# A hybrid streaming encoder step on one core: the last pass over the output visits its tiles in another order, and its norm begins before the pass is over

## The reference, cut to what matters

```
def _rmsnorm(x, g):
    y = xf * lax.rsqrt(jnp.mean(xf * xf, axis=-1, keepdims=True) + EPS)
    return (y * g.astype(jnp.float32)).astype(x.dtype)

    h = _rmsnorm(x, norm1_g) * (1.0 + sc1) + sh1
    mix, new_state = _token_mixers(h, ...)          # h @ w_in, three attentions
    x = x + g1 * (mix @ w_out)
    h = _rmsnorm(x, norm2_g) * (1.0 + sc2) + sh2
    x = x + g2 * (jnp.square(jax.nn.relu(h @ w_up)) @ w_down)
    ...
y_prompt = _rmsnorm(xp, final_g)
```

## Time and profile before

| | us |
|---|---|
| median of 3 runs | 3301.9 (3301.85 to 3302.01) |
| profiled execution | 3300.42 |
| its span | 3298.6 |
| TensorE busy in the span | 3211.7 |
| VectorE busy | 1694.6 |
| ScalarE busy | 984.2 |
| GpSimd busy | 959.5 |

### The profile page before, as it was taken

One profiled execution on the slowest core, in us unless ns is written; L12 is line 12 of the kernel. 1 busy time (PEld: TensorE's weight loads), 2 busy tenths in 40 slices (PEclk: granted clock), 3 DMA queues, 4 the chain that ended last, 5 costly groups with the idle time before them and its releaser, 6 DMA issues.

```text
span 3298.6 us, 50329 instructions
## 1 busy us (share of the span) xinstructions
PE 3211.7 (97%) x19286; PEld 2889.6 (88%) x19286; DVE 1694.6 (51%) x3073; ACT 984.2 (30%) x1770; POOL 959.5 (29%) x690
## 2 busy tenths in 40 slices
PE   6999999999999999999999999999999999999998
PEld 2988898667899999999988879966678999999997
DVE  4746273774485555555663544056546533333335
ACT  3132222764451111111232213157535211111112
POOL 1312333221233333333331215213113233333331
PEclk8999999999999999999999999999999999999999
DMA  5512477545022222222222115554321111111112
GB/s 215 181 43 86 163 240 227 116 111 140 26 71 84 78 88 76 76 83 89 83 65 67 38 47 186 185 144 102 78 70 42 33 46 45 48 47 45 45 45 72
DMA packets 135350, 307.07 MB, mean 93 GB/s; under 512 B 53788, under 2 KB 74340, under 8 KB 131728
## 3 DMA queue, kind: packets, MB, share of 16 engines
q1 hardware_dynamic: 93584, 224.39, 23.3%
q10 hardware_dynamic: 41600, 80.44, 6.9%
HBM read 240.14 MB, written 57.90 MB: 90 GB/s over the span
## 4 chain that ended last, share of the span: by engine, by line
PE 92%; DVE 3%; ACT 1%; ACTq 1%; DMA 1%; issue 1%; POOL 0%; SPq 0%; DVEq 0%; POOLq 0%; PEldq 0%
PE ps L1400 22%; PE ps L1371 19%; PE ps L1312 9%; PE ps L1245 8%; PE ps L1035 6%; PE ps L1225 5%; PE ps L1091 4%; PE ps L1182 3%; PE ps L1289 3%; PE ps L1347 2%; PE ps L1017 2%; PE ps L1059 1%; DVE tn L2066 1%; PE ps L1080 1%; DVE h_lo L2079 1%
## 5 line engine op out<-in xcount | busy, mean ns | idle before, releaser
L781 POOL CAST w_hi<-raw 128x1024 fp32r<-128x1024 f32 x212 | 231.1, 1090 | 1858.5 <-PEq L1406 447.2
L2251 DVE SCALAR_TENSOR_TENSOR x<-ps,mod,x 128x352 f32<-128x352 f32 (+2 forms) x768 | 353.6, 489 | 431.5 <-PE ps L1400 351.5
L1400 PE MATMUL ps<-act_hi,w_hi 128*128 128x352 f32 x1536 | 496.0, 323 | 0.0
L1400 PE MATMUL ps<-act_hi,w_lo 128*128 128x352 f32 x1536 | 492.6, 321 | 0.0
L1400 PE MATMUL ps<-act_lo,w_hi 128*128 128x352 f32 x1536 | 492.1, 320 | 0.0
L1888 ACT ACTIVATE relu_b<-ps,consts 128x352 f32<-128x352 f32 x192 | 106.3, 554 | 1103.5 <-PE ps L1371 1084.4
L1371 PE MATMUL ps<-h_hi,w_hi 128*128 128x352 f32 x1344 | 433.5, 323 | 0.0
L1371 PE MATMUL ps<-h_hi,w_lo 128*128 128x352 f32 x1344 | 430.8, 321 | 0.0
L1371 PE MATMUL ps<-h_lo,w_hi 128*128 128x352 f32 x1344 | 430.4, 320 | 0.0
L1312 PE MATMUL ps<-pT,vb 128*128 128x512 f32 (+5 forms) x1080 | 395.7, 456 | 0.0
L2315 DVE TENSOR_REDUCE pm<-ps 128x1 f32<-128x512 f32 (+4 forms) x468 | 250.2, 547 | 228.3 <-PE ps L1182 144.1
(11 more groups left out here) (223 smaller groups left out, 6095.1 us busy)
## 6 DMA issues: line engine op xcount, KB each, us to landing
raw<-in_w SPq DMA_DIRECT2D x212, 512.0 KB, 3.6
ada_next<-in_w_ada SPq DMA_DIRECT2D x48, 512.0 KB, 4.2
ada_w<-in_w_ada SPq DMA_DIRECT2D x24, 512.0 KB, 4.8
kb<-scr_k SPq DMA_DIRECT2D x36, 328.0 KB
kb<-scr_k SPq DMA_DIRECT2D x120, 82.0 KB
qb<-scr_q SPq DMA_DIRECT2D x36, 264.0 KB
ada_nat<-in_w_ada_first SPq DMA_DIRECT2D x8, 1024.0 KB, 20.4
qb<-scr_q SPq DMA_DIRECT2D x120, 66.0 KB
```

The costliest lines, as they stand in the source:

```text
L781: pool.tensor_copy(hi, raw[:, uc % 2, 0:width]).then_inc(pool_hi, 1)
L1400: last = mm(ps[:, i % 6, 0:GW], w[:, k * 256 + o * 128:k * 256 + o * 128 + 128], (act_lo if low else act_hi)[:, k * T + g * GW:k * T + (g ...
L2251: last = v.scalar_tensor_tensor(xs, ps[:, bank, a - g * GW:b - g * GW], gs, xs, ALU.mult, ALU.add)
```

## The change

The output projection and the last down of each layer use a new order of tiles, `LAST_ORDER`: after blocks 0 to 3, blocks 4 to 7 of group 0 (tiles 12 to 15), then blocks 4 and 5 of groups 1 and 2 (16 to 19), then blocks 6 and 7 of groups 1 and 2 (20 to 23). Group 0 is thus complete at tile 15 instead of 19. TensorE makes its mean of squares behind tile 17 instead of 21, and those of groups 1 and 2 inside the next stage's first group of matmuls. VectorE makes the scalings 0 to 2 and low halves 0 and 1 between the residuals of tiles 19 to 23 (or, after the last layer, six final scalings, and two more around the last add). Weight units are released behind tiles 6, 12, 20 instead of 6, 12, 18, and the unit of blocks 6 and 7 is first used at tile 14 instead of 18. Slots 2 and 5 of the first MLP chunk's units 43 and 44 are exchanged, and GpSimd's split of unit 45 waits for the eighth low half. The modulation products of the last chunk stand at other tiles, its scales at tiles 10 and 12 instead of 15.

```diff
+LAST_ORDER = ([(b, g) for b in range(4) for g in range(GROUPS)] + [(4, 0), (5, 0), (6, 0), (7, 0), (4, 1), (5, 1), (4, 2), (5, 2)] +
+              [(6, 1), (7, 1), (6, 2), (7, 2)])
+RELEASED_AT = (6, 12, 20)
...
-           [2, 0, 1, 2] + [0, 1, 2, 0] + [1, 2, 5, 0, 1, 2, 0, 1])
+           [2, 0, 1, 2] + [0, 1, 2, 0] + [1, 5, 2, 0, 1, 2, 0, 1])
...
-             [(0, i) for i in range(1, 12, 2)] + [(1, i) for i in range(1, 12, 2)]]
+             [(0, i) for i in range(1, 12, 2)] + [(1, i) for i in (1, 2, 3, 5, 7, 8)]]
...
+                    if u == MLP_BASE + 3:
+                        pool.wait_ge(lo_ready, (2 * li + 1) * 24 + KB)
...
             def stat(c, g):
-                pe.wait_ge(sq_added, added(c, 19 + 2 * g))
+                pe.wait_ge(sq_added, added(c, group_at(c, g)))
...
-                        if li and z == 0 and k == 1:
-                            stat(c, 2)
+                        if li and z == 0 and k in (1, 4):
+                            stat(c, 1 if k == 1 else 2)
...
             out_proj
-                for i, (b, g) in enumerate(OUT_ORDER):
-                    if i % 6 == 0:
-                        pe.wait_ge(w_ready, li * NU + OUT1_BASE + i // 6 + 1)
-                    w_of = unit_passes(SLOT_OF[OUT1_BASE + i // 6])
+                for i, (b, g) in enumerate(LAST_ORDER):
+                    if b % 2 == 0 and g == 0:
+                        pe.wait_ge(w_ready, li * NU + OUT1_BASE + b // 2 + 1)
+                    w_of = unit_passes(SLOT_OF[OUT1_BASE + b // 2])
...
-                    if i % 6 == 0 and i:
+                    if i in RELEASED_AT:
                         pe.wait_ge(out_ps, li * 24 + i)
                         pe.sem_inc(w_used, 1)
-                    if i in (21, 23):
-                        stat(2 * li + 1, (i - 21) // 2)
+                    if i == 17:
+                        stat(2 * li + 1, 0)
...
             up_first
-                        if g == 0 and units[0] == 0 and k == 1:
-                            stat(c, 2)
+                        if g == 0 and units[0] == 0 and k in (1, 3):
+                            stat(c, 1 if k == 1 else 2)
...
             squares (ScalarE)
-                for i in range(22):
+                for i in range(18):
                     square(c, i, kept, count)
                 root(c, 0)
-                square(c, 22, kept, count)
-                if c < 2 * L:
-                    high(c, c // 2, c % 2, 0)
-                square(c, 23, kept, count)
-                if c < 2 * L:
-                    for i in range(1, 4):
-                        high(c, c // 2, c % 2, i)
+                for i in range(18, 24):
+                    square(c, i, kept, count)
+                    if c < 2 * L and i in (19, 20, 21):
+                        high(c, c // 2, c % 2, i - 19)
+                if c < 2 * L:
+                    high(c, c // 2, c % 2, 3)
                 root(c, 1)
                 if c < 2 * L:
-                    for i in range(4, 8):
-                        high(c, c // 2, c % 2, i)
+                    high(c, c // 2, c % 2, 4)
+                    high(c, c // 2, c % 2, 5)
                 root(c, 2)
+                if c < 2 * L:
+                    high(c, c // 2, c % 2, 6)
+                    high(c, c // 2, c % 2, 7)
...
             out_proj (VectorE; the last down alike, for the next layer's norm)
+                    if i == 19:
+                        scaled(c, li, 1, 0)
+                    elif i in (20, 21):
+                        normed(c, li, 1, i - 20, i - 19)
-                normed(c, li, 1, 0, 1)
+                normed(c, li, 1, 2, 3)
                 add(c, 23)
-                normed(c, li, 1, 1, 20)
+                normed(c, li, 1, 3, 20)
...
             evicted_down, last layer
+                            for k in {19: (0, 1), 20: (2,), 21: (3, 4), 22: (5,)}.get(i, ()):
+                                final(0, k)
```

More of the change, by code:

```diff
@@ L1382, in down @@
             def down(li, f, n, ub, first, last_one):
-                for i, (b, g) in enumerate(OUT_ORDER):
-                    u, o = i // 6, b % 2
+                for i, (b, g) in enumerate(LAST_ORDER if last_one else OUT_ORDER):
+                    u, o = b // 2, b % 2
                     w_all = unit_passes(SLOT_OF[MLP_BASE + 4 + u] if first else 5 if last_one and u == 3 else u % 2)
-                    if i % 6 == 0:
+                    if b % 2 == 0 and g == 0:
                         pe.wait_ge(w_ready, ub + (u + 5))
@@ L1403, in down @@
                     last.then_inc(down_ps, 1)
-                    if i % 6 == 0:
-                        pe.wait_ge(*((down_ps, n * 24 + i) if i else (up_ps, n * 12 + 12)))
+                    if i == 0:
+                        pe.wait_ge(up_ps, n * 12 + 12)
                         pe.sem_inc(w_used, 1)
-                    if last_one and i in (21, 23):
-                        stat(2 * li + 2, (i - 21) // 2)
+                    if i in (RELEASED_AT if last_one else (6, 12, 18)):
+                        pe.wait_ge(down_ps, n * 24 + i)
+                        pe.sem_inc(w_used, 1)
+                    if last_one and i == 17:
+                        stat(2 * li + 2, 0)
                 if last_one:
@@ L2075, in normed @@
                     if i + 1 < 24:
-                        scaled(i + 1)
+                        scaled(c, li, which, i + 1)
                     dve.wait_ge(hi_ready, c * 24 + (i + 1))
@@ L2503, in _ @@
                 mlp(li)
-            for g in range(GROUPS):
-                dve.wait_ge(rb_ready, 2 * L * 3 + g + 1)
+            for g in range(1, GROUPS):
                 for k in range(KB):
-                    xs = x[:, k * T + g * GW:k * T + (g + 1) * GW]
-                    v.scalar_tensor_tensor(xs, xs, final_g[:, k:k + 1], rb[:, g, :], ALU.mult, ALU.mult).then_inc(
-                        y_ready, 1)
+                    final(g, k)
 def halves_apart():
```

70 lines of the change are left out of this document (44 added, 26 removed).

## The result

The changed kernel takes 3307.99 us (median of 11 runs, 3304.19 to 3311.47) against 3301.9 us of the kernel before (11 runs beside it, 3298.84 to 3305.08): ratio 1.0019, 95% interval 1.0011 to 1.0027. That is 6.1 us slower. I had forecast 3303.2, no change, with a range of 3300 to 3306. A second set of runs gave 3308.47 against 3302.02 (ratio 1.0022, 1.0012 to 1.0031). The profiled execution took 3307.99 us, span 3306.2.

A forecast was written before the change was run, and what follows sets the result against it. VectorE's chain of 24 pieces, not TensorE's start, was taken to bound the output-to-up join. Terms +5.2 - 1.3 - 2.6 = +1.3 us gave 3301.7 against the profiled execution, 3303.2 on the runs; range 3300 to 3306.

The forecast's parts named there:

- What bounds join A: Output projection to up projection, both layers: VectorE's 24 pieces set the end; TensorE's 4.7 us wait is moved, not removed.
- VectorE's end in join A: Output projection to up projection: the last low half comes 0.6 us later (-0.7 + 0.6 + 0.7).
- the root's hold: Output projection to up projection: ScalarE's root of the third mean waits for TensorE's fourth k block, holding high half 6: 0.7 us.
- The other terms: Output projection to up projection, VectorE: filled idle time -0.7 us, GpSimd's splits blocking two-operand instructions +0.6 us.
- The clock: Up projection's thin third group, both layers: TensorE's clock falls and costs 2.0 us, between 0 and 2.4.
- Join A as a whole: Output projection to up projection: 0.6 + 2.0 = 2.6 us later, twice: +5.2 us.
- Join B: Last down of layer 0 to layer 1's projections: -1.3 us, bounds 0 to 3.0.
- add, piece 3, add and five pieces of 1.18 bring low half 7 to 1684.3: Behind layer 0's last down: from residual 23's end at 1676.5, VectorE takes 0.45 + 1.0 + 0.45 + 5.9 us.
- Join C: Last down of layer 1 to the final scaling: -2.6 us, bounds -1.5 and -3.4.
- 3.4 us of stores: Program end: after the last scaling at 3292.5, stores take 3.4 us, to 3295.9.
- The sum: All joins together: +5.2 - 1.3 - 2.6 = +1.3 us.
- Rival R3: Output projection to up projection: VectorE's chain slips, up to 3.4 us a layer; +6.9 us, 3308.8 us; chance 0.12.

The follow-up runs named there:

- experiment 8: Changed kernel, with the fourth unit's tiles of groups 0 and 1 ahead of the third group in both layers' first up projection: 3294.35 us.
- the fillers: Changed kernel plus four more unread TensorE matmuls per k block (28 a layer) in unit 0's third group of the up projection: 3305.59 us.
- Experiment 3: Changed kernel with ScalarE's root of the third mean of squares behind high halves 6 and 7 instead of ahead of them: 3303.88 us.
- experiment 7: Changed kernel with two more of the output's stores, those of the first column group, issued by SyncE instead of ScalarE: 3307.29 us.

## Why the prediction was wrong

- **What bounds join A: right.** "This join is bound by VectorE's chain of 24 pieces" was the main claim, and it held: the early start turned into 14 small waits, and only when TensorE had other work (experiment 8) did it count.
- **VectorE's end in join A: right in sign, small in size.** Forecast 0.6 us later, measured 1.3 and 1.4; with the root late it ends at 2580.33 - 6.35 = 2573.98 in the frame of before, 0.3 later, so the root's hold is worth 1.1 and not the 0.7 that I charged. The other terms, -0.1 in my sum, come to +0.3.
- **The clock: right in kind, large in size.** It fell in the third group in both layers, as forecast, in all seven profiled executions whose third group is thin. The price of 2.0 was too high: the fillers gave some 1.2 to 1.7 back a layer, and 1.4 is what join A has on average beyond VectorE's end. By the rule of the Trainium skill that I cited (TensorE: Matmul & The Clock Gate, section Why this matters for your kernels) the longest gap here, 1.50 us, should have left the clock up; the runs show otherwise.
- **Join A as a whole: right, in part by luck.** Forecast +2.6 a layer; measured +3.0 and +3.4, then +2.7 and +2.5, on average of five executions +2.7 and +2.8. VectorE's term was 0.8 too small and the clock's 0.6 too large.
- **Join B: the step that failed.** Forecast -1.3, measured +1.3. The step was "add, piece 3, add and five pieces of 1.18 bring low half 7 to 1684.3": it let the pieces run free. But ScalarE makes root 2 ahead of high halves 6 and 7, and the third mean is only made behind TensorE's k block 4, which itself waits for low half 4. I had charged that hold in join A and forgot it here. Low half 7 ended at 1691.80 (1686.8 in the frame of before, 5.0 us earlier), 2.5 late on my time. Experiment 3 gives 1.9 us of it back. Residual 23 ended 0.8 us late, at 1677.3 in that frame and not at 1676.5, and the free pieces ran 0.2 faster than I had them.
- **Join C: mis-sized.** Forecast -2.6, measured -1.3 and -0.9. The last scaling was where I had put it (3301.74 less 8.9 is 3292.8, forecast 3292.5); the term "3.4 us of stores" was 4.4. ScalarE's stores of the first group did not start before 3295.70; with two of them on SyncE (experiment 7) the term is 3.1. I had named that as a bound and given it no weight.
- **The sum.** On average joins A together came 0.3 us above the forecast, B 2.6, C 1.3 to 1.7: +5.5 to +6.3 instead of +1.3. So what made the forecast wrong is B and C; join A, which makes most of the loss, was in the sum. Rival R3 (3308.8) has the right time, but not for its reason: it wanted VectorE to slip by some 3.3 us a layer, and it slipped by 1.3 or 1.4.
